# Two norms in front of cross attention: memory's norm is made earlier, and the squares of the second follow the residual chunk by chunk

## The chip, the cores and the metric

One core of a Trainium2 chip runs the whole program. The metric is the device time in microseconds (us) from the first to the last instruction of the slowest core, here of the only one. Five engines work side by side, each with its own instruction stream: TensorE (PE, matmuls into PSUM), VectorE (DVE), ScalarE (ACT), GpSimd (POOL, used here to issue some DMAs) and SyncE (SP, which issues the weight loads). They are kept in step by semaphores only.

## The reference

A layer of two blocks on 256 tokens of width 1024, in float32. The change touches the middle of the first block:

```python
merged = jax.nn.sigmoid(gate_ssd) * y_ssd + jax.nn.sigmoid(gate_mla) * y_mla   # y_mla = o @ w_mla_out
h = h + merged @ w_o[i]
h = h + memory_cross_attention(rms_norm(h, norm_xattn[i]), rms_norm(mem, norm_mem[i]), w_xq[i], w_xkv[i], w_xo[i])
...
def rms_norm(x, gain):
    xf = x * lax.rsqrt(jnp.mean(x * x, axis=-1, keepdims=True) + 1e-6)
    return xf * gain
...
q = h @ w_xq; k, v = jnp.split(mem @ w_xkv, 2, axis=-1)
```

Memory's norm (`n_mem`) doesn't depend on `h`. The norm of cross attention (`n_xattn`) needs the whole of `h` behind `w_o`.

## The kernel before

**Layout.** Activations are held turned: 128 partitions of the width by 8 tiles of the width by 256 tokens (`[128, 8, 256]`). The sum of squares of a norm thus runs over partitions, and a product with a matrix of ones makes it on TensorE (L514 in `norm_sum`), with the sum already spread to all partitions.

**Split weights.** Each weight comes in pieces of 128x2048 (256 output columns of a 1024-row matrix), loaded by SP into one of four `raw` buffers. ScalarE copies it to the reduced format (`whi`, L1325), VectorE subtracts (`wlo`, L1976), and TensorE makes three matmuls for each tile: high by high, high by low, low by high (L457 to L459; L490 to L492 in `chunks_late`). One chunk is 48 matmuls of 128x256. SP loads a piece when the piece four before it is split.

**Order.** Nothing is scheduled at run time: every engine's order is written out by hand, one Python function an engine. `upcoming(name, c)` makes the split of the piece two behind chunk c, on ScalarE and VectorE alike, so that both engines split weights in between their other work. An engine works strictly in its order; a wait stops all behind it.

**The stretch.** TensorE: four chunks of mla_out (the first by `chunks_late`), w_o 0 and 1 together by `chunks_late` (six of eight tiles of both, then the last two tiles, since these come from the last chunk of mla_out), the sum of `n_mem`, w_o 2 and 3, xk 0 (keys from the normed memory), the sum of `n_xattn`, xk 1 to 3, xq 0 to 3. For each chunk of mla_out VectorE multiplies by the gate (L2370), adds the SSD branch (L2372, `G`), ScalarE makes the high part (`MXh`), VectorE the low part (`MXl`, L1982). For each chunk of w_o VectorE adds it to the residual `H` (L2378).

**The norm's helper.** `norm` on ScalarE squares the lower half into `T8` (L1351), makes four gain products (L1325, `T8b`), later Ln and Exp of the sum (L1361, L1363; `table` loads another table set if need be, L1322), and the high part of the normed tiles. On VectorE it squares the upper half (L1991), adds the eight tiles in a tree down to one (L1998), makes the other four gain products (L2005), multiplies by the root (L2015) and makes the low part (L1982). `T8` is also `G2`, the MLA gate, and `T8b` holds keys of MLA, so `n_mem` can start only when the mixing is over; memT, too, is loaded by POOL only then, since its buffer overlaps others.

Of the kernel before, what the change touches and what calls it, by code (L numbers as in the profile page):

```python
# [4 lines left out]
F32 = mybir.dt.float32  # L5
# [3 lines left out]
ALU = mybir.AluOpType  # L9
# [215 lines left out]
def build(nc, I, out, parts, vectors):  # L225
# [36 lines left out]
    def R(name, shape, dt, offset):  # L262
        if name not in made:
            n = 4
            for s in shape[1:]:
                n *= s
            assert offset + n <= size, (name, offset + n, size)
            made[name] = sb(name, shape, dt, rbase + offset)
        return made[name]
# [104 lines left out]
    OAh, OAl = R("OAh", [128, 8, 256], F32R, 66 * KB), R("OAl", [128, 8, 256], F32R, 16 * KB)  # L374
    MXh, MXl = R("MXh", [128, 8, 256], F32R, 34 * KB), R("MXl", [128, 8, 256], F32R, 42 * KB)
    memT = R("memT", [128, 8, 256], F32, 8 * KB)
    MMh, MMl = R("MMh", [128, 8, 256], F32R, 16 * KB), R("MMl", [128, 8, 256], F32R, 24 * KB)
    XVh, XVl = R("XVh", [128, 8, 256], F32R, 32 * KB), R("XVl", [128, 8, 256], F32R, 40 * KB)
    q2, k2 = R("q2", [128, 8, 256], F32, 48 * KB), R("k2", [128, 8, 256], F32, 56 * KB)
# [57 lines left out]
    ru2 = ru[:, :].unsqueeze(1).broadcast_to([128, 2, 256])  # L437
    rh2 = rs[:, 256:512].unsqueeze(1).broadcast_to([128, 2, 256])
    rs2 = rs[:, 0:256].unsqueeze(1).broadcast_to([128, 2, 256])

    def halves(ps, a=2):
        return ps[:, :].rearrange("p (a n) -> p a n", a=a)
# [7 lines left out]
    def pe_program(pe):  # L450
# [56 lines left out]
        def norm_sum(nm, nt, ng=1, banks=bank):  # L507
            ps, free = banks.take(nm, "ms")
            v = T8[:, 0:ng * nt, :].rearrange("p (g k) n -> p g k n", g=ng)
            m = nt if nt % 2 else 1  # L510
            w.wait_ge(*free)
            w.wait_ge(*at_(nm, "squares"))
            for k in range(m):
                t = pe.matmul(ps[:, 0:256 * ng], ones[:, :], v[:, :, k, :], start=k == 0, stop=k == m - 1)  # L514
            t.then_inc(*did("norm_pe", nm, "ms"))
# [256 lines left out]
            chunk("mla_out", c, OAh, OAl, 8, lambda k: at_("emptied", "o", k // 2))  # L772


        def mem_side():
            yield
            norm_sum("n_mem", 8)

        side = mem_side()
        chunks_late("w_o", (0, 1), MXh, MXl, 8, lambda k: at_("mix", "lo", k // 2), 6)  # L780
        next(side)
        next(side, None)
        for c in range(2, 4):
            chunk("w_o", c, MXh, MXl, 8, lambda k: at_("mix", "lo", k // 2))

# [1 line left out]
        for c in range(4):  # L787
            chunk("xk", c, MMh, MMl, 8, lambda k: at_("n_mem", "lo", k // 4))
            if c == 0:
                norm_sum("n_xattn", 8)  # L790
        for c in range(4):
            chunk("xq", c, XVh, XVl, 8, lambda k: at_("n_xattn", "lo", k // 4))
        for j in range(2):
# [521 lines left out]
    def act_program(act):  # L1315
# [307 lines left out]
        for c in range(4):  # L1623
            upcoming("mla_out", c)
            w.wait_ge(*at_("mix", "sum", c))
            copy(MXh[:, 2 * c:2 * c + 2, :], G[:, 2 * c:2 * c + 2, :]).then_inc(*did("mix_act", "mix", "hi", c))

        def mem_side():
            yield from norm("n_mem", memT, 8, 1024, col["norm_mem"], ("dma", "mem"), [("mix", "lo", 3)], hs=MMh)

        side = mem_side()
        for c in range(4):
            upcoming("w_o", c)
            next(side, None)
        finish(side)


        side = norm("n_xattn", H, 8, 1024, col["norm_xattn"], ("emptied", "w_o", 3), [("n_mem", "lo", 1)], hs=XVh)
        next(side)
        for c in range(4):  # L1640
            upcoming("xk", c)
            evac(k2[:, 2 * c:2 * c + 2, :], "xk", c)
            next(side, None)
        finish(side)
        for c in range(4):
            upcoming("xq", c)
            evac(q2[:, 2 * c:2 * c + 2, :], "xq", c)
# [314 lines left out]
    def dve_program(dve):  # L1962
# [402 lines left out]
        for c in range(4):  # L2365
            upcoming("mla_out", c)
            f = slice(2 * c, 2 * c + 2)
            w.wait_ge(*at_("used", first["mla_out"] + c))
            w.wait_ge(*at_("mix", "sig2"))
            dve.tensor_tensor(G2[:, f, :], G2[:, f, :], halves(bank.ps("mla_out", c)), ALU.mult).then_inc(*bank.emptied("mla_out", c))  # L2370
            w.wait_ge(*at_("emptied", "mla_out", c))
            dve.tensor_tensor(G[:, f, :], G[:, f, :], G2[:, f, :], ALU.add).then_inc(*did("mix_dve", "mix", "sum", c))  # L2372
            w.wait_ge(*at_("mix", "hi", c))
            rest(MXl[:, f, :], G[:, f, :], MXh[:, f, :]).then_inc(*did("mix_dve", "mix", "lo", c))

        def residual(name, c):
            w.wait_ge(*at_("used", first[name] + c))
            dve.tensor_tensor(H[:, 2 * c:2 * c + 2, :], H[:, 2 * c:2 * c + 2, :], halves(bank.ps(name, c)), ALU.add).then_inc(*bank.emptied(name, c))  # L2378

        side = norm("n_mem", memT, 8, 1024, col["norm_mem"], T8b, ("dma", "mem"), [], hl=(MMh, MMl))  # L2380
        for c in range(4):
            upcoming("w_o", c)
            residual("w_o", c)
            next(side, None)
        finish(side)


        side = norm("n_xattn", H, 8, 1024, col["norm_xattn"], T8b, ("emptied", "w_o", 3), [], hl=(XVh, XVl))
        next(side)
        for c in range(4):  # L2390
            upcoming("xk", c)
            next(side, None)
        finish(side)
        for c in range(4):
            upcoming("xq", c)
        for j in range(2):
# [482 lines left out]
    def pool_program(pool):  # L2879
# [31 lines left out]
        pool.memset(kn[1][0:64, :, :], 0.0).then_inc(*did("mla_pool"))  # L2911
        w.wait_ge(*now("mla_pool"))
        pool.memset(kpm[:, :, :], 0.0).then_inc(*did("mla_pool", "mla", "zero"))
        w.wait_ge(*at_("mix", "lo", 3))
        pool.dma_start(memT[:, :, :], I["c_mem"].rearrange("p (k n) -> p k n", k=8)).then_inc(*did("mem", "dma", "mem", by=16))
        w.wait_ge(*at_("used", first["xv"] + 3))
        pool.dma_start(wr[:, :, :], I["c_router"].rearrange("p (k n) -> p k n", k=8)).then_inc(*did("router", "dma", "router", by=16))
# [91 lines left out]
```

## Time and profile before

| | |
|---|---|
| median of 3 runs | 1107.22 us (1103.17 to 1111.86) |
| the profiled execution, first to last instruction | 1106.8 us |
| mean granted TensorE clock | 0.974 of full speed |
| TensorE busy | 1021.5 us, 92% |
| VectorE busy | 622.6 us, 56% |
| ScalarE busy | 516.9 us, 47% |
| HBM read | 238.58 MB, 217 GB/s over the span |

The profile and the runs agree, so that a stretch of the trace can be added to or taken from the median. TensorE's share is the largest, but it is an average over stages; in some of them (the experts) it waits for weights.

### The profile page before, as it was taken

Reading aid. Unit: us, or ns where it says so; the run is one execution under the profiler, and the core shown is the slowest. Engines: PE = TensorE matmul, PEld = TensorE weight load, DVE = VectorE, ACT = ScalarE, POOL = GpSimd, SP = SyncE. Lnnn points to the kernel's source line nnn. Section 1 sums busy time; section 2 is a strip of 40 time slices with the busy share of each in tenths; the row PEclk is TensorE's granted clock in tenths of the full one; section 3 lists DMA queues with packets and bytes.
Section 4 is the critical chain, followed back from the end, with each engine's and each line's share of the span. In section 5 each row is a group of like instructions: output and inputs, shape, how many; then the busy total and the mean of one; then the engine's idle time right before and its main releaser. Section 6 shows DMA issues by size and latency. Waiting matters only on the chain.

```text
span 1106.8 us, 19429 instructions
## 1 busy us (share of the span) xinstructions
PE 1021.5 (92%) x8574; PEld 941.1 (85%) x8574; DVE 622.6 (56%) x828; ACT 516.9 (47%) x701; POOL 19.4 (2%) x24
## 2 busy tenths in 40 slices
PE   7999989899999899999997676788999999999998
PEld 6999978899889899899665443478999999999998
DVE  6887677765565784544111101068994665545566
ACT  5576576745555554442211110158566564443443
POOL 0000020001000000000000000000000000000000
PEclk9999999999999899998998888899999999999999
DMA  7665343446223555299999999964430355555441
GB/s 279 231 242 191 137 155 115 150 150 238 80 77 115 193 188 191 99 365 406 384 420 421 420 420 421 420 267 157 162 114 11 153 213 206 190 191 190 163 143 39
DMA packets 34871, 240.96 MB, mean 218 GB/s; under 512 B 4064, under 2 KB 4448, under 8 KB 6368
## 3 DMA queue, kind: packets, MB, share of 16 engines
q1 hardware_dynamic: 33264, 232.54, 55.1%
q0 software_dynamic: 1232, 6.99, 1.8%
q8 instruction: 70, 1.15, 0.4%
q10 hardware_dynamic: 288, 0.15, 0.1%
q14 instruction: 17, 0.14, 0.0%
HBM read 238.58 MB, written 1.08 MB: 217 GB/s over the span
## 4 chain that ended last, share of the span: by engine, by line
PE 68%; DVE 12%; DMA 9%; ACT 7%; issue 3%; SPq 2%; DVEq 0%; ACTq 0%
PE ps L457 15%; PE ps L459 15%; PE ps L458 15%; DVE wlo L1976 4%; PE ps L530 4%; PE ps L1226 4%; DMA xlo<-in_c_weights 3%; ACT whi L1325 3%; DMA xhi<-in_c_weights 3%; DMA wr<-in_c_weights 2%; PE ps L1192 2%; SPq L2933 2%; PE ps L1253 1%; PE ps L1266 1%; PE ps L929 1%
## 5 line engine op out<-in xcount | busy, mean ns | idle before, releaser
L1976 DVE TENSOR_TENSOR wlo<-raw,whi 128x2048 fp32r<-128x2048 f32 (+1 forms) x119 | 269.5, 2266 | 141.1 <-ACT whi L1325 141.1
L457 PE MATMUL ps<-XUh,whi 128*128 128x256 f32 x992 | 282.3, 285 | 9.2 <-DVE wlo L1976 8.4
L459 PE MATMUL ps<-XUh,wlo 128*128 128x256 f32 x992 | 278.3, 281 | 0.0
L458 PE MATMUL ps<-XUl,whi 128*128 128x256 f32 x992 | 278.2, 280 | 0.0
L1325 ACT ACTIVATE whi<-raw 128x2048 fp32r<-128x2048 f32 (+1 forms) x119 | 223.5, 1880 | 61.9 <-PE ps L459 61.9
L457 PEld LDWEIGHTS ps<-XUh,whi 128*128 128x128 f32 x992 | 187.3, 189 | 11.3 <-issue 7.7
L459 PEld LDWEIGHTS ps<-XUh,wlo 128*128 128x128 f32 x992 | 189.4, 191 | 0.0
L458 PEld LDWEIGHTS ps<-XUl,whi 128*128 128x128 f32 x992 | 187.5, 189 | 0.3
L1226 PE MATMUL ps<-wr,Xg 128*32 128x256 f32 x464 | 57.6, 433 | 6.2 <-DMA wr<-in_c_weights 4.6
L2855 DVE SCALAR_TENSOR_TENSOR sphs<-sphs,wsl,ps 128x256 f32<-128x256 f32 x8 | 3.8, 480 | 99.0 <-ACT sphs L1941 99.0
L1941 ACT ACTIVATE sphs<-ps 128x256 f32<-128x256 f32 x8 | 3.1, 383 | 102.1 <-PE ps L1226 102.1
L457 PE MATMUL ps<-ffnah,whi 128*128 128x256 f32 x176 | 49.4, 281 | 0.7 <-DVE wlo L1976 0.7
L459 PE MATMUL ps<-ffnah,wlo 128*128 128x256 f32 x176 | 49.1, 279 | 0.0
L458 PE MATMUL ps<-ffnal,whi 128*128 128x256 f32 x176 | 49.1, 279 | 0.0
L1226 PE MATMUL ps<-raw,Xg 128*32 128x256 f32 x208 | 37.9, 455 | 11.5 <-DMA wr<-in_c_weights 7.5
L1226 PEld LDWEIGHTS ps<-wr,Xg 128*32 128x32 f32 x464 | 29.5, 124 | 14.6 <-issue 9.2
L457 PE MATMUL ps<-YAh,whi 128*128 128x256 f32 x128 | 37.0, 289 | 2.3 <-DVE YAl L1982 2.3
L458 PE MATMUL ps<-YAl,whi 128*128 128x256 f32 x128 | 36.3, 284 | 0.0
L459 PE MATMUL ps<-YAh,wlo 128*128 128x256 f32 x128 | 36.3, 284 | 0.0
L1226 PEld LDWEIGHTS ps<-raw,Xg 128*32 128x32 f32 x208 | 17.5, 130 | 20.1 <-issue 17.2
L457 PEld LDWEIGHTS ps<-ffnah,whi 128*128 128x128 f32 x176 | 33.0, 188 | 0.8 <-issue 0.8
L459 PEld LDWEIGHTS ps<-ffnah,wlo 128*128 128x128 f32 x176 | 33.1, 188 | 0.0
(619 smaller groups left out, 2377.4 us busy)
## 6 DMA issues: line engine op xcount, KB each, us to landing
raw<-in_c_weights SPq DMA_DIRECT2D x141, 1024.0 KB, 4.9
wr<-in_c_weights SPq DMA_DIRECT2D x42, 1024.0 KB, 26.4
xhi<-in_c_weights SPq DMA_DIRECT2D x13, 1024.0 KB, 26.1
xlo<-in_c_weights SPq DMA_DIRECT2D x13, 1024.0 KB, 26.3
acb<-sums POOLq DMA_DIRECT2D x4, 1024.0 KB, 5.1
T<-in_c_weights SPq DMA_DIRECT2D x4, 1024.0 KB, 26.8
T8b<-in_c_weights SPq DMA_DIRECT2D x4, 1024.0 KB, 26.4
raw<-in_c_weights SPq DMA_DIRECT2D x4, 576.0 KB, 3.7
```

Source lines behind the costliest of these rows:

```text
L457: pe.matmul(ps, h(k), xh(k), start=start and k == 0, stop=False, skip_group_check=loose)
L458: pe.matmul(ps, h(k), xl(k), start=False, stop=False, skip_group_check=loose)
L459: t = pe.matmul(ps, l(k), xh(k), start=False, stop=stop and k == kt - 1, skip_group_check=loose)
L530: t = pe.matmul(ps[:, 256 * j:256 * j + 256], wt[:, k, 128 * j:128 * j + 128], x[:, k, :], start=n == j == 0, stop=n == 7, skip_group_chec ...
L929: t = pe.matmul(ps[:, 128 * hd:128 * hd + 128], x, x)
L1192: t = pe.matmul(ps[:, 128 * r:128 * r + 128], XT[:, j, 128 * k:128 * k + 128], Pg[:, j, :], start=j == 0, stop=j == 1)
L1226: t = pe.matmul(ps[o:o + 32, 256 * n:256 * n + 256], Xg[:, k, o:o + 32], plain_of(expert[name, 4 * g + e])[:, k, :], start=k == 0, stop=k ...
L1253: t = pe.matmul(dps[f][o:o + 32, :], aT[:, k, o:o + 32], plain_of(i)[:, k, 512 * f:512 * f + 512], start=k == 0, stop=k == 1)
L1266: t = pe.matmul(ps, Y[:, c], PT[:, :], start=g == 0 and d % 2 == 0, stop=False, skip_group_check=True)
L1325: return act.activation(out, in_, ACT.Copy, **kw)
L1976: dve.tensor_tensor(l[:, 0:n], r, h[:, 0:n].bitcast(F32), ALU.subtract).then_inc(*did("w_lo", "split", i))
L2933: sp.dma_start(raw_of(i), I["c_weights"][o:o + 128 * kt * n].rearrange("(p n) -> p n", p=128)).then_inc(*did("%s%d" % home[i], "loaded", i ...
```

## The change

- POOL issues memT's DMA behind the last transposes of MLA (`pT` 3) and not behind the last `MXl`.
- Two new tiles lie in the space of `XUh`, free once gate_mla is through: `memsq` for the squares of memory, `memg` for memory times its gain.
- ScalarE squares memory in mla_out's turns 0 and 1 (two 128x512 squares in each) and makes the eight gain products in turns 2 and 3 (four 128x256 in each). VectorE adds squares behind `MXl` in turns 1 and 2 (`add_square`, 128x512) and stops at two tiles.
- TensorE sums these two tiles by two products (`row_sum`), ahead of w_o 0 and 1. ScalarE takes the root ahead of the w_o loop and so of the split of w_o 2.
- In w_o's loop ScalarE makes memory's high part in turn 0, and in each turn c, behind the residual c, one square of 128x512 of `H` and two gain products. VectorE multiplies memory by the root in turn 0, makes its low part in turn 1, and adds squares of `H` in turns 2 and 3 and once behind the loop.
- The sum of `n_xattn` stays behind xk 0 and is two products as well. Its root, high and low part are made in the turns of xk 0 and xk 1.

```diff
 # tiles
+    memsq, memg = sb("memsq", [128, 8, 256], F32, xu_at), sb("memg", [128, 8, 256], F32, xu_at + 8 * KB)
 # TensorE
-        def mem_side():
-            yield
-            norm_sum("n_mem", 8)
-
-        side = mem_side()
+        def acc_sum(nm, acc):
+            ps, free = bank.take(nm, "ms")
+            w.wait_ge(*free)
+            row_sum(nm, ps[:, 0:256], acc).then_inc(*did("norm_pe", nm, "ms"))
+
+        acc_sum("n_mem", memsq)
         chunks_late("w_o", (0, 1), MXh, MXl, 8, lambda k: at_("mix", "lo", k // 2), 6)
-        next(side)
-        next(side, None)
...
             if c == 0:
-                norm_sum("n_xattn", 8)
+                acc_sum("n_xattn", T8)
 # ScalarE
             copy(MXh[:, 2 * c:2 * c + 2, :], G[:, 2 * c:2 * c + 2, :]).then_inc(*did("mix_act", "mix", "hi", c))
+            w.wait_ge(*at_("dma", "mem"))
+            w.wait_ge(*at_("used", first["gate_mla"] + 3))
+            if c < 2:
+                for j in (2 * c, 2 * c + 1):
+                    square("n_mem", memsq, memT[:, 2 * j:2 * j + 2, :], j)
+            else:
+                for k in range(4 * c - 8, 4 * c - 4):
+                    t = copy(memg[:, k, :], memT[:, k, :], scale=col["norm_mem"][:, k:k + 1])
+                t.then_inc(*did("norm_act", "n_mem", "gain", c - 2))
+
+        def upper(nm, hs, src):
+            for i in range(2):
+                w.wait_ge(*at_(nm, "dst", i))
+                copy(hs[:, 4 * i:4 * i + 4, :], src[:, 4 * i:4 * i + 4, :]).then_inc(*did("norm_act", nm, "hi", i))
+
+        root("n_mem", rs[:, 0:256], bank)
         for c in range(4):
             upcoming("w_o", c)
-            next(side, None)
+            if c == 0:
+                upper("n_mem", MMh, memg)
+            w.wait_ge(*at_("emptied", "w_o", c))
+            square("n_xattn", T8, H[:, 2 * c:2 * c + 2, :], c)
+            for k in (2 * c, 2 * c + 1):
+                t = copy(T8b[:, k, :], H[:, k, :], scale=col["norm_xattn"][:, k:k + 1])
+            t.then_inc(*did("norm_act", "n_xattn", "gain", c))
         for c in range(4):
             upcoming("xk", c)
             evac(k2[:, 2 * c:2 * c + 2, :], "xk", c)
-            next(side, None)
+            if c == 0:
+                root("n_xattn", rs[:, 256:512], bank)
+            if c == 1:
+                upper("n_xattn", XVh, T8b)
 # VectorE
             rest(MXl[:, f, :], G[:, f, :], MXh[:, f, :]).then_inc(*did("mix_dve", "mix", "lo", c))
+            if c == 1:
+                w.wait_ge(*at_("n_mem", "sq", 0))
+                add_square("n_mem", memsq, 1)
+            if c == 2:
+                add_square("n_mem", memsq, 2)
+                add_square("n_mem", memsq, 3)
...
         for c in range(4):
             upcoming("w_o", c)
+            if c == 0:
+                scale("n_mem", memg, rs4)
             residual("w_o", c)
-            next(side, None)
+            if c == 1:
+                lower("n_mem", MMl, memg, MMh)
+                w.wait_ge(*at_("n_xattn", "sq", 0))
+            if c > 1:
+                add_square("n_xattn", T8, c - 1)
+        add_square("n_xattn", T8, 3)
         for c in range(4):
             upcoming("xk", c)
+            if c == 1:
+                scale("n_xattn", T8b, rh4)
+                lower("n_xattn", XVl, T8b, XVh)
 # POOL
-        w.wait_ge(*at_("mix", "lo", 3))
+        w.wait_ge(*at_("pT", 3))
         pool.dma_start(memT[:, :, :], I["c_mem"].rearrange("p (k n) -> p k n", k=8)).then_inc(*did("mem", "dma", "mem", by=16))
```

`scale` multiplies by the root in two halves of 128x1024, `lower` subtracts the high part in two halves. `add_square`, `square`, `row_sum` and `root` are helpers of the kernel before, printed above where the diff calls them.

## Rows read from the trace of the kernel before

**Rows 1.** The page: busy time by engine, and the chain that ended last by engine

```profile
PE 1021.5 (92%) x8574; PEld 941.1 (85%) x8574; DVE 622.6 (56%) x828; ACT 516.9 (47%) x701; POOL 19.4 (2%) x24
...
PE 68%; DVE 12%; DMA 9%; ACT 7%; issue 3%; SPq 2%; DVEq 0%; ACTq 0%
```

**Rows 2.** Waits in 340 to 450: who waited for whom, us, times, longest

```profile
POOL memT L2915 <- DVE MXl L1982: 110.6, 1, 110.6
...
PE ps L514 <- DVE T L1998: 5.6, 2, 4.3
```

**Rows 3.** Windows: length, PE, PEld, DVE, ACT, POOL busy, granted clock, DMA share, GB/s

```profile
350.30:367.30 17.00, 17.00 (x147) 17.00 (x146) 12.48 (x12) 5.95 (x7) 0.00 (x0) 1.00 0.43 142
...
378.85:383.08 4.23, 0.00 (x0) 0.03 (x1) 3.71 (x5) 3.76 (x6) 0.00 (x0) 0.78 0.55 227
383.08:397.15 14.07, 14.07 (x98) 13.89 (x99) 11.39 (x9) 8.17 (x8) 0.00 (x0) 0.82 0.43 150
388.00:389.00 1.00, 1.00 (x10) 1.00 (x10) 1.00 (x1) 0.00 (x0) 0.00 (x0) 0.98 0.70 295
...
404.35:427.20 22.85, 22.85 (x192) 22.80 (x193) 16.98 (x10) 13.09 (x13) 0.00 (x0) 1.00 0.53 186
448.00:452.00 4.00, 4.00 (x20) 3.51 (x20) 2.68 (x4) 0.04 (x1) 0.00 (x0) 1.00 0.02 6
```

**Rows 4.** ScalarE in order of time: start, us, engine, line, what, idle before

```profile
354.58 1.90 ACT L1325 ACTIVATE whi<-raw 128x2048 fp32r<-128x2048 f32 x1
...
372.41 0.63 ACT L1325 ACTIVATE MXh<-G 128x512 fp32r<-128x512 f32 x1 [3.68 <-DVE G L2372]
372.94 1.90 ACT L1325 ACTIVATE whi<-raw 128x2048 fp32r<-128x2048 f32 x1
379.32 1.06 ACT L1351 ACTIVATE T<-memT 128x1024 f32<-128x1024 f32 x1 [4.48 <-DMA memT<-in_c_mem]
380.28 1.69 ACT L1325 ACTIVATE T8b<-memT,vec 128x256 f32<-128x256 f32 x4
381.88 1.89 ACT L1325 ACTIVATE whi<-raw 128x2048 fp32r<-128x2048 f32 x1
383.79 1.28 ACT L1322 ACT_TABLE_LOAD   x1
385.09 0.47 ACT L1361 ACTIVATE rs<-ps,small 128x256 f32<-128x256 f32 x1
...
385.92 1.89 ACT L1325 ACTIVATE whi<-raw 128x2048 fp32r<-128x2048 f32 x1
```

**Rows 5.** VectorE in order of time

```profile
356.52 2.29 DVE L1976 TENSOR_TENSOR wlo<-raw,whi 128x2048 fp32r<-128x2048 f32 x1 [1.11 <-ACT whi L1325]
...
366.95 0.69 DVE L1982 TENSOR_TENSOR MXl<-G,MXh 128x512 fp32r<-128x512 f32 x1 [0.70 <-ACT MXh L1325]
368.75 2.29 DVE L1976 TENSOR_TENSOR wlo<-raw,whi 128x2048 fp32r<-128x2048 f32 x1 [1.11 <-ACT whi L1325]
370.96 0.68 DVE L2370 TENSOR_TENSOR T<-T,ps 128x512 f32<-128x512 f32 x1
371.68 0.69 DVE L2372 TENSOR_TENSOR G<-G,T 128x512 f32<-128x512 f32 x1
...
392.32 2.35 DVE L2015 TENSOR_TENSOR T8b<-T8b,rs 128x1024 f32<-128x1024 f32 x2
```

**Rows 6.** The chain that ended last at memT's DMA; TensorE behind the second sum

```profile
374.07 5.17 DMA memT<-in_c_mem
...
404.35 0.67 PE L514 MATMUL ps<-T,ones 128*128 128x256 f32 x2 [1.36 <-DVE T L1998]
404.67 0.47 PE L457 MATMUL ps<-MMh,whi 128*128 128x256 f32 x1
```

**Rows 7.** A wait of TensorE in MLA, and a window behind it

```profile
333.13 0.46 PE L746 MATMUL ps<-PT,V 128*64 128x256 f32 x2 [2.33 <-ACT PT L1325]
...
334.00:336.00 2.00, 2.00 (x15) 1.44 (x12) 1.49 (x2) 1.51 (x3) 0.00 (x0) 0.50 0.00 0
```

More of the change, by code:

```diff
@@ L439, in build @@
     rs2 = rs[:, 0:256].unsqueeze(1).broadcast_to([128, 2, 256])
+    rs4, rh4 = (rs[:, o:o + 256].unsqueeze(1).broadcast_to([128, 4, 256]) for o in (0, 256))
     def halves(ps, a=2):
@@ L1626, in act_program @@
             copy(MXh[:, 2 * c:2 * c + 2, :], G[:, 2 * c:2 * c + 2, :]).then_inc(*did("mix_act", "mix", "hi", c))
-        def mem_side():
-            yield from norm("n_mem", memT, 8, 1024, col["norm_mem"], ("dma", "mem"), [("mix", "lo", 3)], hs=MMh)
-        side = mem_side()
+            w.wait_ge(*at_("dma", "mem"))
[12 more added lines that the diff above has]
+        root("n_mem", rs[:, 0:256], bank)
         for c in range(4):
             upcoming("w_o", c)
-            next(side, None)
-        finish(side)
-        side = norm("n_xattn", H, 8, 1024, col["norm_xattn"], ("emptied", "w_o", 3), [("n_mem", "lo", 1)], hs=XVh)
-        next(side)
+            if c == 0:
[5 more added lines that the diff above has]
+            t.then_inc(*did("norm_act", "n_xattn", "gain", c))
         for c in range(4):
@@ L1642, in act_program @@
             evac(k2[:, 2 * c:2 * c + 2, :], "xk", c)
-            next(side, None)
-        finish(side)
+            if c == 0:
+                root("n_xattn", rs[:, 256:512], bank)
+            if c == 1:
+                upper("n_xattn", XVh, T8b)
         for c in range(4):
@@ L2378, in residual, with scale, lower @@
             dve.tensor_tensor(H[:, 2 * c:2 * c + 2, :], H[:, 2 * c:2 * c + 2, :], halves(bank.ps(name, c)), ALU.add).then_inc(*bank.emptied(name, c))
-        side = norm("n_mem", memT, 8, 1024, col["norm_mem"], T8b, ("dma", "mem"), [], hl=(MMh, MMl))
+        def scale(nm, x, r4):
+            w.wait_ge(*at_(nm, "r"))
+            for i in range(2):
+                f = slice(4 * i, 4 * i + 4)
+                w.wait_ge(*at_(nm, "gain", i if nm == "n_mem" else 3))
+                dve.tensor_tensor(x[:, f, :], x[:, f, :], r4, ALU.mult).then_inc(*did("norm_dve", nm, "dst", i))
+        def lower(nm, l, x, h):
+            for i in range(2):
+                f = slice(4 * i, 4 * i + 4)
+                w.wait_ge(*at_(nm, "hi", i))
+                rest(l[:, f, :], x[:, f, :], h[:, f, :]).then_inc(*did("norm_dve", nm, "lo", i))
         for c in range(4):
             upcoming("w_o", c)
+            if c == 0:
+                scale("n_mem", memg, rs4)
             residual("w_o", c)
-            next(side, None)
-        finish(side)
-        side = norm("n_xattn", H, 8, 1024, col["norm_xattn"], T8b, ("emptied", "w_o", 3), [], hl=(XVh, XVl))
-        next(side)
+            if c == 1:
[4 more added lines that the diff above has]
+        add_square("n_xattn", T8, 3)
         for c in range(4):
             upcoming("xk", c)
-            next(side, None)
-        finish(side)
+            if c == 1:
+                scale("n_xattn", T8b, rh4)
+                lower("n_xattn", XVl, T8b, XVh)
         for c in range(4):
```

## The prediction

> **What bounds the kernel now.** I read the page first: TensorE is busy 92% of the span, and the chain that ended last is 68% TensorE with 12% VectorE, 9% DMA and 7% ScalarE [rows 1]. So only what TensorE waits for counts, and the question is which waits lie in the stretch that the diff touches (350 to 450 us) and what ends them. The list of waits names TensorE's own two: both are L514, the product that sums the squares of a norm, 5.6 us in total, and behind it stands the POOL queue, which issues the DMA of memT only after the last `MXl` [rows 2]. The windows then price them. TensorE runs without a gap from 350.3 to 378.85; it is empty until 383.08; it runs again, but the granted clock has fallen to its lower level of 1.2 GHz and returns at 388; a second gap of 1.36 us stands before `n_xattn`'s sum [rows 6]; from 404.35 to 427.2 it is full again [rows 3]. Full means 48 matmuls a chunk at 0.1177 us each, 5.65 us (three mla_out chunks take the 17.0 us of row 350.30).
>
> Next the other two engines, since the change moves work onto them. In the mla_out loop the two are not free, though their shares look low. ScalarE's `whi` of the next weight waits behind `MXh`, which waits for `G`, which on VectorE stands behind the `wlo` of the weight before. One turn is: `whi` to `wlo` 1.94 (354.58 to 356.52), `wlo` to the gate product 2.21 (368.75 to 370.96), from there to `G` 0.72, `G` to `MXh` 0.73, `MXh` to `whi` 0.53, together 6.13 us. The `wlo` rows 356.52 and 368.75 stand two turns of 6.12 apart [rows 4, 5]. TensorE's turn is 5.65 us. **The loop that looks half idle is a closed chain already slower than TensorE**; TensorE hides it only because the splits run ahead. w_o 1 is split at 368.75 + 2.29 = 371.04, and TensorE, in w_o 0 from 367.3, wants it 36 matmuls later at 371.5.
>
> **What is removed.** memT's DMA (5.2 us from issue to landing) moves from 374.07 to behind the last transposes of MLA [rows 6]. Between those and 350.3 lie two chunks (11.3) and the last value products, so it is issued near 338 and landed by 344, ten us before its first reader; POOL has nothing between, and behind it the DMA engines' share is 0.43 [rows 3], so I cost it at nothing. Were a weight late by it, `whi` would wait for its load, at most for its 5.2 us. The wait of 4.23 us goes, with it the slow clock after it: 383.08 to 397.15 is 14.07 us for one sum (0.5, below) and 96 matmuls (11.3), so the clock cost 2.3 us. The wait of 1.36 us before `n_xattn`'s sum would go too, if the squares kept up. Those are 7.9 us. VectorE also loses its squares, its gain product and the wide tree additions, but where they stood TensorE was waiting or VectorE had time.
>
> **What is added on TensorE.** Each sum becomes two products instead of one. L514 has two records for one product, 0.67 us together [rows 6]; less the tail that any matmul lays over the next (0.28 - 0.12) that is 0.5 us. So +0.5 twice, 1.0 us. The gain is then at most 7.9 - 1.0 = 6.9 us.
>
> **What is added to the chain.** Prices from rows 4: a square of 128x512 isn't there; the copy `MXh` of the same shape from SBUF is 0.63 us, 0.53 to the next start; half of L1351 (1.06 for 128x1024, 0.96 to the next start) gives 0.48. Bounds are 0.40 (a 128x256 step) and 0.63 (no overlap). Four gain copies take 1.60 to the next start (380.28 to 381.88).
> Turn 0: two squares in front of `whi`, +1.06. Turn 1: two more, +1.06, 2.12 in all. So `MXl` of turn 2 starts at 366.95 + 2.12 = 369.07. Behind it VectorE makes the additions 2 and 3 (a 128x512 addition like `G`, 0.69; the second waits for the first): 369.67 and 370.39, done 371.08. **The new order on TensorE puts `n_mem`'s sum ahead of w_o 0 and 1**, which are ready at 367.3. What is queued behind this wait is 96 matmuls that need nothing from it. TensorE idles 367.3 to 371.1, 3.8 us: the removed wait is back, 11 us earlier, for another reason.
> Turns 2 and 3: four gain copies each, +1.60 each. `MXh` of turn 3 comes at 372.41 + 2.12 + 1.60 = 376.13; then 0.53, the copies 1.60, and the root, which now stands in front of `whi` of w_o 2: table load 1.30, Ln 0.50, Exp 0.33 (383.79 to 385.92). `whi` of w_o 2 starts at 380.39; before it was 372.94. Split at 380.39 + 1.94 + 2.29 = 384.6. TensorE, from 371.1, has 1.0 + 11.3 and arrives at 383.4: 1.2 us idle.
> w_o loop: behind that split VectorE scales memory (L2015's two halves, 2.35), then the residual 0 (a 128x512 operation like the gate product, 386.84 to 387.52). ScalarE makes both upper halves (until 387.9), a square 0.53 and two gains 0.80, and `whi` of w_o 3 starts at 389.3; split at 393.5. TensorE finished w_o 2 at 390.3: 3.2 us idle. From here each turn is `whi` 1.94, `wlo` 2.21, residual 0.71, square 0.53, gains 0.80, 6.19 us, again closed, since the gains of chunk c stand before the `whi` of the weight after next. `whi` of xk 0 at 395.5, split 399.7 (idle 0.5); `whi` of xk 1 at 401.7; residual 3 at 405.85, its square at 406.56, the last addition 407.2 to 407.9. TensorE ended xk 0 at 405.4, so 2.5 us idle, then the two products. xk 1 starts at 408.9. Before it started at 404.67 [rows 3, 6].
>
> The sum: waits 3.8 + 1.2 + 3.2 + 0.5 + 2.5 = 11.2 and four products 2.0, 13.2 us, against 5.6 + 1.0 + 2.3 = 8.9 before, +4.3; the two starts give **+4.2 us**, which I take. Eight squares stand in the chain; with steps of 0.40 or 0.63 instead of 0.53 it is +3.2 or +5.0. Behind xk 1 nothing changes: carried on by the same durations, the splits of xk 2, xk 3 and `XVl` fall at 412, 415 and 420 against needs at 414.4, 420 and 425.7, TensorE is full, and later DMAs start from events that move along (in 448 to 452 the DMA share is 0.02) [rows 3]. So the shift reaches the end whole.
>
> On the table load row 383.79 shows 1.28 us and the Ln starts 0.02 us later, and that is what I used. The Trainium skill (ScalarE: Activation LUTs, "What ACT_TABLE_LOAD costs") adds a drain, about 2.66 us in all, to a switch. As the root now stands in the chain, that would make the sum +5.6 instead of +4.2; this trace does not show the drain.
>
> **Rivals.**
> A, a gain: the added work on ScalarE and VectorE fits in their idle time. For it speaks that both are idle a third of the loop and more, that all squares are off TensorE and that the DMA is out of the way. Then xk 1 starts at 367.3 + 1.0 + 22.6 + 5.65 + 1.0 = 397.55, 7.1 us earlier: 1100.1 us. Against it speaks the 6.12 us turn. It can come true only in part, by as much as ScalarE gets ahead; the idle 3.68 us before each `MXh` ends with `G`, thus with the chain itself. Half of it would be 1103.7.
> B, slower through the clock: the lower level after waits. A wait of 2.33 us was followed by a stretch at 0.50 of full speed, the one of 4.23 by a longer one, that of 1.36 by none [rows 3, 6, 7]. Here 3.8, 3.2 and 2.5 us waits stand in a row. The first two cost little, for TensorE waits for splits behind them anyway (a slow w_o 3 would end by 402 and xk 0 with the sum's due time). The place that decides is the wait of 2.5 us before `n_xattn`'s sum: behind it TensorE is the bound, and a stretch at half clock there is not hidden. Price by the stretch of before 2.3 us: +6.5, 1113.7 us. If the clock slows w_o 3, this last wait shrinks to some 1.3 us and the fall may not come, which is why B is not my forecast.
> On rule B the Trainium skill (TensorE: Matmul & The Clock Gate, "HAM oscillation — how this bites in real kernels") says that waits in each tile bring the slow clock back each time; the rows here agree for the longer waits and not for the one of 1.36.
> C, the change doesn't act (the sum's wait stays where the DMA ended it): excluded by the order of the POOL queue; I give it nothing of its own.
>
> **How the numbers follow.** The profiled execution spans 1106.8 us, the median of the runs is 1107.22 (1103.17 to 1111.86), so the two agree and I add to the median: 1107.2 + 4.2 = 1111.4. Chances: forecast (+3 to +5.5) 0.52; B, with whatever small misses lengthen the chain (+5.5 to +9), 0.22; a partial gain or nothing (-4 to +3) 0.12; A whole 0.07; worse than +9, by a chain that I don't see, 0.07. One per cent, 11 us, is about what a measurement of this kernel can tell from no change. A whole is -0.7%, so even there faster by over 1% needs luck: 0.04. Over +11 us: 0.06. The rest 0.90. The range for 8 in 10 leaves out A and the worst: 1102 to 1117.
>
> **What would show it.** In the profile after: memT landing near 344; TensorE empty from about 367 to 371 and released by a VectorE addition; `wlo` rows 7.2, 7.2, 7.7 us apart in the mla_out loop instead of 6.12, and three waits of L457 for `wlo`, of which that for w_o 3 is over 3 us; then about 2.5 us before the second sum; xk 1 at 408 to 409. If instead the wait at 367 is under 1 us, my closed turn is wrong and A holds. If all starts agree and the time is longer, it is the granted clock behind 408. What would make all of it wrong is a release that I put on the wrong instruction, above all whether `whi` really stands behind the squares in ScalarE's order.

## The result and the profile after

The changed kernel takes 1111.35 us (median of 20 runs, 1104.64 to 1116.53), the kernel before in the same rounds 1105.32 us: a ratio of 1.0042, 95% interval 1.0025 to 1.0058. The change makes the kernel slower by 0.4%, which is 4.6 us with an interval of 2.8 to 6.4 us. (The two medians alone stand 6.0 us apart.) The profiled execution of the changed kernel spans 1111.7 us, against 1106.8.

The page first (busy time by engine, then the chain that ended last). TensorE is busy 3.2 us longer and ScalarE 5.7 us, VectorE 5.9 us less. These totals over the whole span don't say where the 4.9 us of span come from; ScalarE's part of the last chain rises from 7% to 9% [rows 1].

```profile
PE 1024.7 (92%) x8578; PEld 942.5 (85%) x8578; DVE 616.7 (55%) x824; ACT 522.6 (47%) x715; POOL 19.4 (2%) x24
...
PE 65%; DVE 12%; DMA 11%; ACT 9%; issue 3%; SPq 1%; DVEq 0%; ACTq 0%
```

Who waited for whom in 340 to 450, the answer to [rows 2] (L539 is the matmul of `row_sum`, which takes L514's place; L459 is the former L457, L1993 the former L1976):

```profile
DVE wlo L1993 <- ACT whi L1326: 43.2, 17, 4.9
...
PE ps L539 <- DVE memsq L2054: 3.8, 1, 3.8
...
PE ps L539 <- DVE T L2054: 2.3, 1, 2.3
...
PE ps L459 <- DVE wlo L1993: 1.5, 1, 1.5
```

Both sums still wait, and a wait for a split weight has joined them. VectorE's waits for `whi` stood at 29.3 us in this list before (15 times) and are now 43.2 us (17 times): the additional work of ScalarE is seen there, though two more waits are in the count. Windows of the same stretch, the answer to [rows 3]:

```profile
366.07:369.83 3.76, 0.01 (x1) 0.03 (x1) 2.78 (x5) 2.90 (x6) 0.00 (x0) 0.91 0.82 279
369.83:376.00 6.17, 6.17 (x25) 5.81 (x26) 4.27 (x4) 2.49 (x5) 0.00 (x0) 0.50 0.28 77
376.00:382.80 6.80, 6.80 (x59) 6.80 (x59) 1.86 (x1) 4.85 (x7) 0.00 (x0) 1.00 0.20 84
382.80:390.74 7.94, 7.94 (x68) 7.74 (x66) 4.29 (x5) 5.25 (x6) 0.00 (x0) 1.00 0.38 134
390.74:392.20 1.46, 0.00 (x1) 0.03 (x1) 1.46 (x2) 0.00 (x0) 0.00 (x0) 1.00 0.00 0
...
404.32:406.66 2.34, 0.00 (x1) 0.03 (x1) 2.09 (x4) 1.51 (x4) 0.00 (x0) 1.00 0.54 102
406.66:410.20 3.54, 3.54 (x13) 3.18 (x14) 1.79 (x1) 3.51 (x5) 0.00 (x0) 0.52 0.55 229
```

Read the columns PE and PEclk together. TensorE is empty for 3.76 us ahead of w_o, then works 6.2 us at half clock; it is empty for 1.46 us before w_o 3 and for 2.34 us before the second sum, and then works at half clock again for some 3.4 us. ScalarE in order of time, the answer to [rows 4], shows the turns of mla_out:

```profile
352.62 0.63 ACT L1326 ACTIVATE MXh<-G 128x512 fp32r<-128x512 f32 x1 [3.69 <-DVE G L2389]
353.15 1.14 ACT L1376 ACTIVATE memsq<-memT 128x512 f32<-128x512 f32 x2
354.19 1.90 ACT L1326 ACTIVATE whi<-raw 128x2048 fp32r<-128x2048 f32 x1
359.78 0.63 ACT L1326 ACTIVATE MXh<-G 128x512 fp32r<-128x512 f32 x1 [3.68 <-DVE G L2389]
...
366.93 0.63 ACT L1326 ACTIVATE MXh<-G 128x512 fp32r<-128x512 f32 x1 [3.68 <-DVE G L2389]
...
374.64 0.63 ACT L1326 ACTIVATE MXh<-G 128x512 fp32r<-128x512 f32 x1 [3.68 <-DVE G L2389]
375.18 1.69 ACT L1326 ACTIVATE memg<-memT,vec 128x256 f32<-128x256 f32 x4
376.89 1.28 ACT L1323 ACT_TABLE_LOAD   x1
378.18 0.47 ACT L1381 ACTIVATE rs<-ps,small 128x256 f32<-128x256 f32 x1
378.69 0.42 ACT L1383 ACTIVATE rs<-rs 128x256 f32<-128x256 f32 x1
379.01 1.90 ACT L1326 ACTIVATE whi<-raw 128x2048 fp32r<-128x2048 f32 x1
```

The squares take 1.04 us from their start to that of `whi`, the four gain products behind the third `MXh` 1.59, and **the idle time before each `MXh` is still 3.68 us**. ScalarE was idle for 3.68 us a turn, took on 1.0 to 1.6 us of work a turn, and is idle for 3.68 us a turn: the turn has become longer by the work. That is the mark of a closed chain. VectorE's rows say the same, the answer to [rows 5] (`wlo` at 348.96, 356.13, 363.29, 370.99; turns of 7.17, 7.16 and 7.70 us instead of 6.12):

```profile
348.96 2.29 DVE L1993 TENSOR_TENSOR wlo<-raw,whi 128x2048 fp32r<-128x2048 f32 x1 [4.34 <-ACT whi L1326]
...
356.13 2.29 DVE L1993 TENSOR_TENSOR wlo<-raw,whi 128x2048 fp32r<-128x2048 f32 x1 [2.15 <-ACT whi L1326]
...
363.29 2.29 DVE L1993 TENSOR_TENSOR wlo<-raw,whi 128x2048 fp32r<-128x2048 f32 x1 [1.55 <-ACT whi L1326]
...
368.21 1.48 DVE L2054 TENSOR_TENSOR memsq<-memsq 128x512 f32<-128x512 f32 x2
370.99 2.29 DVE L1993 TENSOR_TENSOR wlo<-raw,whi 128x2048 fp32r<-128x2048 f32 x1 [1.30 <-ACT whi L1326]
```

The chain that ended last, in order of time, runs through exactly these instructions between 360 and 371, with no TensorE in it:

```profile
360.31 1.14 ACT memsq L1376 x2
361.45 1.81 ACT whi L1326
363.26 0.02 issue
363.29 2.29 DVE wlo L1993
365.58 0.60 DVE T L2387
366.19 0.02 issue
366.21 0.70 DVE G L2389
```

**One stretch for all comparisons.** Runs of one kernel differ by up to 1%, and what happens ahead of 350 us is not the change's doing, so I compare by a stretch: from the start of the first `MXh` to the start of ScalarE's eviction of xk 1, the first point behind which TensorE is again the bound. Before it is 410.71 - 354.05 = 56.66 us, after 415.06 - 352.62 = 62.44 us: +5.8 us in this execution, of which 1.7 is the fall of the clock behind the second sum (half of 3.4 us). The other 4.1 are what the longer waits, the two further products and the slow clock behind the first wait add. The span shows 4.9, since in this execution the changed kernel reached the first `MXh` 1.4 us earlier. It was 0.9 us ahead at 21 us already and gained another 0.5 near 213 us, where its clock stayed at full speed while that of before fell behind a wait of 2.3 us. The code there is the same. Behind xk 1 both have the same way to go (696.1 and 696.6 us).

### The profile page after: what moved, and what is told of

Its sections match the earlier page's. It is cut to its first block, busy times and chain, and to the rows that moved or that the text cites. A ratio compares the mean times of both kernels' runs of the same rounds, so it can differ in the third digit from the quotient of the medians.

```text
span 1111.7 us, 19448 instructions
## 1 busy us (share of the span) xinstructions
PE 1024.7 (92%) x8578; PEld 942.5 (85%) x8578; DVE 616.7 (55%) x824; ACT 522.6 (47%) x715; POOL 19.4 (2%) x24
## 4 chain that ended last, share of the span: by engine, by line
PE 65%; DVE 12%; DMA 11%; ACT 9%; issue 3%; SPq 1%; DVEq 0%; ACTq 0%
PE ps L459 15%; PE ps L461 14%; PE ps L460 14%; DMA raw<-in_c_weights 6%; DVE wlo L1993 5%; PE ps L532 4%; PE ps L1227 3%; ACT whi L1326 3%; DMA xhi<-in_c_weights 3%; DMA wr<-in_c_weights 2%; PE ps L1193 1%; PE ps L930 1%; PE ps L1254 1%; PE ps L1267 1%; PE ps L825 1%
## 5 line engine op out<-in xcount | busy, mean ns | idle before, releaser
L1993 DVE TENSOR_TENSOR wlo<-raw,whi 128x2048 fp32r<-128x2048 f32 (+1 forms) x119 | 269.6, 2267 | 154.3 <-ACT whi L1326 154.2
L459 PE MATMUL ps<-XUh,whi 128*128 128x256 f32 x992 | 281.4, 284 | 8.8 <-DVE wlo L1993 8.2
L459 PEld LDWEIGHTS ps<-XUh,whi 128*128 128x128 f32 x992 | 186.6, 188 | 10.7 <-issue 7.4
L1227 PE MATMUL ps<-wr,Xg 128*32 128x256 f32 x464 | 55.3, 426 | 6.6 <-DMA wr<-in_c_weights 4.7
L459 PE MATMUL ps<-ffnah,whi 128*128 128x256 f32 x176 | 49.4, 281 | 0.7 <-DVE wlo L1993 0.7
L1227 PE MATMUL ps<-raw,Xg 128*32 128x256 f32 x208 | 37.3, 450 | 13.3 <-DMA wr<-in_c_weights 9.2
L459 PE MATMUL ps<-YAh,whi 128*128 128x256 f32 x128 | 36.3, 284 | 2.8 <-DVE YAl L1999 2.2
L459 PEld LDWEIGHTS ps<-ffnah,whi 128*128 128x128 f32 x176 | 33.0, 188 | 0.8 <-issue 0.8
```

Source lines behind the costliest of these rows:

```text
L459: pe.matmul(ps, h(k), xh(k), start=start and k == 0, stop=False, skip_group_check=loose)
L1227: t = pe.matmul(ps[o:o + 32, 256 * n:256 * n + 256], Xg[:, k, o:o + 32], plain_of(expert[name, 4 * g + e])[:, k, :], start=k == 0, stop=k ...
L1993: dve.tensor_tensor(l[:, 0:n], r, h[:, 0:n].bitcast(F32), ALU.subtract).then_inc(*did("w_lo", "split", i))
```

## The experiments

Times of different rounds lie up to 5 us apart for one kernel, so ratios to the kernel before in the same rounds are given (8 to 12 runs of each experiment, 20 of the changed kernel); the stretch is that just defined, from the one profiled execution of each. Where the clock fell behind the last wait in that execution (changed, e2, e5, e9), the stretch holds some 1.7 us for it.

| kernel | ratio to before (95%) | stretch, us |
|---|---|---|
| before | 1 | 56.66 |
| changed | 1.0042 (1.0025 to 1.0058) | 62.44 |
| e1: memory's work ahead of the wait | 0.9991 (0.9965 to 1.0017) | 55.76 |
| e2: sum behind w_o 0 and 1 | 1.0090 (1.0055 to 1.0124) | 65.78 |
| e3: before, with the early DMA | 0.9987 (0.9959 to 1.0015) | 55.82 |
| e4: rearranged | 0.9927 (0.9902 to 0.9951) | 49.15 |
| e5: changed, first wait filled | 1.0042 (1.0022 to 1.0062) | 62.38 |
| e6: changed, last wait filled | 1.0025 (1.0005 to 1.0045) | 61.23 |
| e7: memory part alone | 0.9994 (0.9970 to 1.0017) | 56.81 |
| e8: rearranged, one product a sum | 0.9928 (0.9904 to 0.9952) | 49.10 |
| e9: rearranged in memory's part only | 0.9999 (0.9981 to 1.0016) | 55.07 |
| e10: changed, squares doubled | a single run, 1114.29 us | 62.90 |
| e11: e1, squares doubled | a single run, 1107.47 us | 55.77 |

**e1: memory's squares and gains ahead of the wait for the mix sum.**

```diff
             upcoming("mla_out", c)
-            w.wait_ge(*at_("mix", "sum", c))
-            copy(MXh[:, 2 * c:2 * c + 2, :], G[:, 2 * c:2 * c + 2, :]).then_inc(*did("mix_act", "mix", "hi", c))
             w.wait_ge(*at_("dma", "mem"))
             w.wait_ge(*at_("used", first["gate_mla"] + 3))
             if c < 2:
...
                 t.then_inc(*did("norm_act", "n_mem", "gain", c - 2))
+            w.wait_ge(*at_("mix", "sum", c))
+            copy(MXh[:, 2 * c:2 * c + 2, :], G[:, 2 * c:2 * c + 2, :]).then_inc(*did("mix_act", "mix", "hi", c))
```

> The changed kernel with one thing moved: in mla_out's turns ScalarE makes memory's squares and gain products ahead of its wait for the mix sum (where it sat idle 3.68 us in each turn) and not behind the high part of the mix. Same work, same sums, same place of the sum on TensorE. Closed chain (my theory): the turns fall back from 7.2, 7.2, 7.7 us to 6.12; the wait before n_mem's sum shrinks from 3.8 to about 1.7 us, the start of xk 1 comes 5.2 us earlier than in the changed kernel, so about 1.2 us earlier than before the change: ratio to before 0.999, with 2.5 us still waited before the second sum. Rival, the place of the sum on TensorE: the place is the same, so the time stays at +4 to +5 us over before. Rival, the amount of work on ScalarE and VectorE: the same, so also +4 to +5.

Measured: ratio 0.9991; the `wlo` rows stand 6.12, 6.13 and 6.32 us apart, the wait before the sum is 1.68 us:

```profile
370.01 1.10 PE L539 MATMUL ps<-memsq,ones 128*128 128x256 f32 x4 [1.68 <-DVE memsq L2054]
```

The same instructions, swapped with one copy and its wait, take the whole loss away: the interval of e1 ends at 1.0017, that of the changed kernel begins at 1.0025. Of the 6.7 us of stretch between the two, 1.7 is the fall of the clock, which did not come in e1's execution; 5.0 are left, against 5.2 expected. Neither the amount of work nor the place of the sum, which are the same in both, makes the loss by itself.

**e2: the sum back to its old place on TensorE.**

```diff
-        acc_sum("n_mem", memsq)
         chunks_late("w_o", (0, 1), MXh, MXl, 8, lambda k: at_("mix", "lo", k // 2), 6)
+        acc_sum("n_mem", memsq)
```

> The changed kernel with n_mem's sum moved on TensorE behind w_o 0 and 1, where it was before the change; ScalarE's order stays, with the root ahead of the split of w_o 2. Closed chain: the wait of 3.8 us goes, but the root now ends near 385 and with it every later split comes later; TensorE waits over 5 us for w_o 2 and 3.3 us for w_o 3, xk 1 starts 3.5 us later than in the changed kernel: +7.5 to +9 us over before, ratio 1.007 to 1.008. Rival, the place of the sum on TensorE: the wait of 3.8 us is gone and nothing replaces it, +0 to +1 us over before.

Measured: ratio 1.0090, stretch +3.3 us on the changed kernel. The place of the sum looks like the culprit in the list of waits (3.8 us, the longest), and moving it makes things worse. Its removal uncovers the next release: ScalarE's root now waits for the sum and holds up `whi` of w_o 2 behind it, from 379.01 to 382.26, and TensorE waits 6.6 us for two splits: 5.14 us for w_o 2, and 1.45 for w_o 3 where 3.3 were expected, with a stretch at half clock in between. ScalarE of e2 in order of time:

```profile
376.75 1.28 ACT L1323 ACT_TABLE_LOAD   x1
381.43 0.47 ACT L1381 ACTIVATE rs<-ps,small 128x256 f32<-128x256 f32 x1 [3.40 <-PE ps L539]
381.94 0.42 ACT L1383 ACTIVATE rs<-rs 128x256 f32<-128x256 f32 x1
382.26 1.89 ACT L1326 ACTIVATE whi<-raw 128x2048 fp32r<-128x2048 f32 x1
```

**e3: the early DMA alone, in the kernel before.**

```diff
-        w.wait_ge(*at_("mix", "lo", 3))
+        w.wait_ge(*at_("pT", 3))
         pool.dma_start(memT[:, :, :], I["c_mem"].rearrange("p (k n) -> p k n", k=8)).then_inc(*did("mem", "dma", "mem", by=16))
```

> The kernel before with one line of the change: memT is loaded behind the last transposes of MLA. Its norm still runs in w_o's loop. My reckoning: the squares start at 378.1 (VectorE, behind the residual) instead of 379.3, the sum 1.1 us earlier, the wait 3.1 instead of 4.2 us, and nothing is late by the earlier load: -1 us, ratio 0.999; with the clock falling for 3.4 instead of 6.8 us it is up to -2.7. Rival, the early load costs by contention with weights: 0 or slower than before.

Measured: ratio 0.9987, stretch -0.84 us, the waits for both sums 4.4 us instead of 5.6. One line of the change, taken alone, costs nothing; that it gains in time stays within the interval, the stretch shows its size.

**e4: the same work rearranged.** ScalarE's loop over mla_out and over w_o, and VectorE's additions:

```diff
             upcoming("mla_out", c)
+            if c == 0:
+                w.wait_ge(*at_("dma", "mem"))
+                w.wait_ge(*at_("used", first["gate_mla"] + 3))
+                for j in range(4):
+                    square("n_mem", memsq, memT[:, 2 * j:2 * j + 2, :], j)
+            elif c < 3:
+                for k in range(4 * c - 4, 4 * c):
+                    t = copy(memg[:, k, :], memT[:, k, :], scale=col["norm_mem"][:, k:k + 1])
+                t.then_inc(*did("norm_act", "n_mem", "gain", c - 1))
+            else:
+                root("n_mem", rs[:, 0:256], bank)
             w.wait_ge(*at_("mix", "sum", c))
             copy(MXh[:, 2 * c:2 * c + 2, :], G[:, 2 * c:2 * c + 2, :]).then_inc(*did("mix_act", "mix", "hi", c))
...
-        root("n_mem", rs[:, 0:256], bank)
         for c in range(4):
             upcoming("w_o", c)
+            if c:
+                follow(c - 1)
             if c == 0:
                 upper("n_mem", MMh, memg)
-            w.wait_ge(*at_("emptied", "w_o", c))
-            square("n_xattn", T8, H[:, 2 * c:2 * c + 2, :], c)
...
+        follow(3)
```

`follow(c)` is the wait for residual c, its square and its two gains. On VectorE the additions stand behind turns 0 and 1.

> All of the change's work in other places of ScalarE's and VectorE's order: the four squares of memory ahead of the wait for the mix sum in turn 0, the gain products in turns 1 and 2, the root in turn 3; VectorE's three additions behind turns 0 and 1; in w_o's loop the square and gains of residual c stand behind the split made in turn c+1. Closed chain: no wait is left between 350 and xk 1, xk 1 starts 11.4 us earlier than in the changed kernel, 7.3 us earlier than before: ratio to before 0.993 (0.992 to 0.995). Rival, the amount of work: it is the same as in the changed kernel, so +4 to +5 us. Rival, the place of the sum on TensorE (unchanged): its wait ends when the squares end, so a gain of at most 3.8 us on the changed kernel: 0.

Measured: ratio 0.9927. **TensorE waits for nothing between 350 and xk 1's end**, the granted clock is 1.00 throughout, and the stretch is 7.5 us shorter than before (7.3 expected) and 13.3 shorter than in the changed kernel (11.4 expected, which left out the clock fall of 1.7 behind the changed kernel's last wait). ScalarE of e4 in the first turns; the work lies in front of `MXh`, and the idle time has shrunk by it, as it should where work is covered:

```profile
349.40 2.18 ACT L1376 ACTIVATE memsq<-memT 128x512 f32<-128x512 f32 x4
353.18 0.63 ACT L1326 ACTIVATE MXh<-G 128x512 fp32r<-128x512 f32 x1 [1.60 <-DVE G L2396]
353.71 1.90 ACT L1326 ACTIVATE whi<-raw 128x2048 fp32r<-128x2048 f32 x1
355.52 1.69 ACT L1326 ACTIVATE memg<-memT,vec 128x256 f32<-128x256 f32 x4
359.30 0.63 ACT L1326 ACTIVATE MXh<-G 128x512 fp32r<-128x512 f32 x1 [2.09 <-DVE G L2396]
```

**e5 and e6: products of ones in a wait, to hold the clock.** They add work that nobody reads, in front of one of the sums:

```diff
             w.wait_ge(*free)
+            if nm == "n_mem":                                   # e5; e6: "n_xattn" and 9 products
+                constant_products(pe, ps[:, 384:512], 14)
             row_sum(nm, ps[:, 0:256], acc).then_inc(*did("norm_pe", nm, "ms"))
```

> The changed kernel with 14 products of ones (128x128) on TensorE in its first wait (3.8 us), ahead of n_mem's sum, into an unused part of the bank; nothing reads them. They take some 3.1 us and keep TensorE's clock from falling. Theory: the time that the slow clock costs behind the first wait is hidden, since TensorE waits for the splits of w_o 2 and 3 anyway; the waits that the slow clock had swallowed come back (about 1.2 us before w_o 2, 3.2 us before w_o 3) and xk 1 starts where it did: no change against the changed kernel, ratio to before 1.004. Rival, the clock is the cost: w_o 0 to 2 run at full speed, some 2.3 us are saved at the end, ratio 1.002.

Measured: ratio 1.0042, the same as the changed kernel, stretch 62.38. The clock stayed at full speed through w_o, as this window of e5 shows (PEclk 1.00 where the changed kernel had 0.50), and the time that this saved came back as waits for splits.

```profile
367.50:376.00 8.50, 8.50 (x69) 8.40 (x70) 4.27 (x4) 4.79 (x8) 0.00 (x0) 1.00 0.35 125
```

These waits are 4.1 us in all instead of 1.5, the one before w_o 3 is 2.98 us instead of 1.46, as TensorE's row of e5 has it:

```profile
389.93 0.36 PE L459 MATMUL ps<-MXh,whi 128*128 128x256 f32 x1 [2.98 <-DVE wlo L1995]
```

Here the slow clock in front of a later wait cost nothing.

> The changed kernel with 9 products of ones (128x128, about 2.0 us) in the last of its waits (2.3 us, before n_xattn's sum). Behind this wait TensorE is the bound, and the profile after showed 3.4 us at 1.2 GHz there. If that fall is a cost of its own: 1.7 us less than the changed kernel from the last high part of the mix to the end of xk 1 (60.8 us instead of 62.4), ratio to before 1.0027 against 1.0042. If the fall cost nothing: no change.

Measured: stretch 61.23 instead of the 60.8 expected (w_o 3 ran at half clock in this execution, xk 0 ended 0.8 us later, and the products, 2.17 us, ran 0.5 us over the sum's due time), ratio 1.0025 against 1.0042. The intervals of the two overlap, so in time it is not shown; in the stretch 1.2 of the 1.7 us are back, with no fall behind the sum. The profiled executions show the price directly: from the start of xk 0's eviction to that of xk 1's it is 6.78, 6.71 and 6.72 us where the clock fell (changed, e5, e9) and 5.16, 5.16 and 5.17 where it didn't (e1, e10, e11), behind the same wait of 2.34 us. A slow clock behind the last wait does cost.

**e7: memory's part alone.** n_xattn's norm is that of before (`norm` on ScalarE and VectorE, `norm_sum` on TensorE):

```diff
-                acc_sum("n_xattn", T8)
+                norm_sum("n_xattn", 8)
...
-            w.wait_ge(*at_("emptied", "w_o", c))
-            square("n_xattn", T8, H[:, 2 * c:2 * c + 2, :], c)
...
+        side = norm("n_xattn", H, 8, 1024, col["norm_xattn"], ("emptied", "w_o", 3), [("n_mem", "lo", 1)], hs=XVh)
...
```

> The memory part of the change alone; n_xattn's norm as before (squares behind the whole residual, a tree, one product). Closed chain: the wait of 3.8 us and the split of w_o 2 stay as in the changed kernel, but w_o's turns lose the square and the gains (1.33 us a turn), the wait for w_o 3's split is 1.9 instead of 3.3, the wait before the second sum 0.9, xk 1 starts 3.9 us earlier than in the changed kernel: ratio to before 1.000 to 1.001. Thus both halves of the change cost about the same. Rival, only the place of n_mem's sum costs: the time stays at 1.004.

Measured: ratio 0.9994, stretch 56.81, 5.6 us less than the changed kernel (3.9, and no clock fall, as the last wait is 0.63 us). The wait of 3.76 us before n_mem's sum is still there, so a kernel with that wait in full is as fast as the one before. Put on top of e7, the residual's part of the change, squares in front of the next split, brings 5.6 of the 5.8 us (1.7 of them the fall of the clock); the equal halves of the expectation did not come. But e1 takes as much away by touching memory's part alone. The waits stand in a row, so the parts don't add up to shares of the loss.

**e8: the rearranged kernel with one product a sum.** VectorE adds the two remaining tiles (`last_add`, 128x256) and TensorE makes one product of the result.

> The rearranged kernel (memory's work ahead of the waits, residual squares one split later) with each sum as one product, VectorE adding the last two tiles first (128x256, 0.44 us, in its slack). If a product costs 0.5 us of TensorE where nothing else waits: 1.0 us less than the rearranged kernel, ratio to before 0.992. If VectorE's additional addition makes a wait, it shows before L539's place: then no gain.

Measured: ratio 0.9928, stretch 49.10, no gain. TensorE saves 0.43 us at the first sum (from its start to w_o 0's first product 0.24 us instead of 0.67) and then waits 0.57 us for w_o 3's split, where it waited for nothing. VectorE's rows show why. Here is turn 1 of e4:

```profile
360.57 1.48 DVE L2061 TENSOR_TENSOR memsq<-memsq 128x512 f32<-128x512 f32 x2
361.97 2.28 DVE L2000 TENSOR_TENSOR wlo<-raw,whi 128x2048 fp32r<-128x2048 f32 x1
```

and here the same place in e8:

```profile
359.85 1.48 DVE L2062 TENSOR_TENSOR memsq<-memsq 128x512 f32<-128x512 f32 x2
361.37 0.42 DVE L2068 TENSOR_TENSOR memsq<-memsq 128x256 f32<-128x256 f32 x1
361.71 2.29 DVE L2001 TENSOR_TENSOR wlo<-raw,whi 128x2048 fp32r<-128x2048 f32 x1
```

In e4 VectorE has no idle time before this `wlo`. In e8 it therefore starts 9.26 us behind the first `MXh` instead of 8.79, and the `wlo` of w_o 3 28.99 instead of 28.51. The added 0.42 us lie in the closed chain and make it longer. The second sum saves its 0.44 us (from its start to xk 1's eviction 6.28 us instead of 6.72), which make up for that and no more.

**e9: only memory's part rearranged.** As e4, but the squares and gains of the residual stay ahead of the next split.

> Between the changed and the rearranged kernel: memory's squares, gain products and root ahead of the waits as in the rearranged one, but in w_o's loop the square and gains of residual c still ahead of the split of the next weight, as in the changed one. Closed chain: no wait before n_mem's sum and w_o 2; w_o's turns stay at 6.2 us, so waits of about 1.0 us for w_o 3, 0.5 for xk 0 and 2.5 before the second sum stay, xk 1 starts 7.3 us earlier than in the changed kernel and 4.1 later than in the rearranged one; from the first high part of the mix to the end of xk 1 53.4 us, and 55.1 if the clock falls behind the last wait; ratio to before 0.997. Rival, what is left of the cost lies in memory's part alone: as fast as the rearranged kernel, 0.993.

Measured: ratio 0.9999, stretch 55.07 (55.1 expected with the clock fall, which came), waits 1.0, 0.3 and 2.34 us. The ratio is above the 0.997 that I expected. That had left out the fall, which is 1.7 us or 0.0015, about half of the miss; 0.9985 lies in the interval, and the rest stays open. Against e4 one difference is left, the place of `follow`, and it is worth 5.9 us of stretch, 1.7 of them the fall of the clock. The `wlo` rows of w_o's loop in e9 stand 6.27 and 6.19 us apart (378.01, 384.28, 390.47), nearly as those of the changed kernel do (6.27 and 6.20): w_o's loop is a second closed chain.

**e10 and e11: each of memory's squares made twice,** behind `MXh` (as in the change) and ahead of the wait (as in e1):

```diff
                 for j in (2 * c, 2 * c + 1):
+                    act.activation(memg[:, 2 * j:2 * j + 2, :], memT[:, 2 * j:2 * j + 2, :], ACT.Square)
                     square("n_mem", memsq, memT[:, 2 * j:2 * j + 2, :], j)
```

> The changed kernel with each of memory's four squares made twice (the additional one into a tile that is overwritten later), in the same place, behind the high part of the mix. Closed chain: each additional square of 0.53 lengthens the chain by itself, two in turn 0 and two in turn 1, 2.1 us: the wait before n_mem's sum is 5.9 us instead of 3.8, the end of xk 1 at 64.5 us from the first high part instead of 62.4. Rival, ScalarE has idle time for it (3.68 us in each turn): no change.

Measured: turns of 8.2, 8.2 and 7.7 us (`wlo` at 346.90, 355.11, 363.31, 371.01), the wait before the sum 5.8 us. The start of xk 0's eviction is 57.74 us from the first `MXh` against 55.66 in the changed kernel, +2.08, as expected. The end of xk 1 is at 62.90, only +0.46: behind the same last wait of 2.34 us the clock did not fall this time (1.00 from 406.67 to 410).

> The same doubled squares in the kernel with memory's work ahead of the wait for the mix sum. Closed chain: four squares, 2.1 us, still fit in the 3.68 us: turns stay at 6.12 us, the wait before n_mem's sum stays 1.7 us, the end of xk 1 at 55.8 us from the first high part, as without them. Rival, the amount of work on ScalarE: 2.1 us later.

Measured: 55.77 us against 55.76 in e1. The same four squares cost 2.1 us behind the high part and nothing in front of the wait. ScalarE's idle time before the first two `MXh` tells the two apart: it is 3.68 us in e10, as without the additional squares, and 1.60 in e11, where e1 has 2.64 and 2.65.

## Why the prediction was right

The forecast was 1111.4 us with xk 1 4.2 us later; it came to 1111.35 and a ratio of 1.0042. That the two times agree to 0.05 us is luck. The forecast was added to a median of 1107.22, and the same kernel measures 1105.32 in the rounds of the result: against that the changed kernel is 6.0 us slower by the medians and 4.6 (2.8 to 6.4) by the ratio. In the profiled execution xk 1 starts 55.48 us behind the first `MXh` instead of 50.62, +4.9. What was right is the chain and the size of its cost. Point by point:

- **The closed turn.** The step on which all hangs, that ScalarE's idle 3.68 us in front of `MXh` are not free for work placed behind it, is shown by e1, by the doubled squares of e10 and e11 and by the `wlo` rows at 7.17, 7.16 and 7.70 us (7.2, 7.2, 7.7 forecast). Prices: two squares took 1.04 to 1.05 us (1.06 forecast from `MXh`), the four gains 1.59, the switch with the root 2.12.
- **The first wait** came as computed, 3.76 us (3.8), released by VectorE's addition.
- **The waits behind it.** Forecast were 1.2 before w_o 2, 3.2 before w_o 3 and 0.5 before xk 0; seen were none, 1.46 and 0.33, so the sign given for w_o 3, over 3 us, did not come. The clock fell to 1.2 GHz behind the first wait for 6.8 us, made w_o 0 to 2 later and so filled the waits. e5, without the fall, has the others: 4.1 us in two, 2.98 of them before w_o 3. That these two exchange without changing the time was a step of rival B, and e5 shows it.
- **The last wait** 2.34 us (2.5). From the first `MXh` on, the second sum starts at 54.04 us; forecast were 407.9 - 354.05 = 53.85.
- **Rival B.** The text gave it as less likely, since a slow w_o 3 would shrink the last wait. In the profiled execution w_o 3 ran at full clock, the last wait stayed long and the clock fell behind it (in e6's it was the other way round): 1.7 us instead of the 2.3 of its price. The cost over 20 runs, 4.6 us with an interval of 2.8 to 6.4, fits the 4.2 without the fall as well as the 5.8 of the profiled execution. How often the fall comes in them was not measured.
- **Rival A** was refuted for this order of instructions and is true of another one. It was priced at 1100.1 us, 0.9936 of before; e4, with the same work, measures 0.9927. Its reasoning on the amount of idle time was sound; what failed it was the place of the work, as the prediction had it. The prediction's sentence that it could come true only in part holds for the change, not for the kernel.
- **The removed DMA wait, at nothing for the early load:** it landed in 7.7 us instead of 5.2, near 344, and held up nobody; e3 shows it alone.
- **The table switch** cost what its row shows: 1.28 us and 0.01 to the Ln, in the chain (376.89 to 378.18). The drain of which the Trainium skill speaks (ScalarE: Activation LUTs, "What ACT_TABLE_LOAD costs"), which by the prediction's estimate would have made it +5.6, did not appear: the page's figure doesn't hold here.
- **The second product of each sum** was priced at 0.5 us. e4 and e8 differ by it and show 0.43 us at the first sum and 0.44 at the second, at full clock. e8 gained nothing since VectorE's addition, put in its place, stands in the closed chain.

Not tried was the residual's part alone on the kernel before; its share follows from e7 and e9 by subtraction only.

## What to carry to other kernels

Idle time in front of a wait is free only for work placed in front of that wait. Put the same work behind the instruction that the wait guards, and in a loop in which two engines release each other, as here, the turn gets longer by all of it, while the idle time in the profile stays as it was: an engine that took on work and is idle exactly as long as before sits in such a chain. Work given to the other engine of such a loop is no better off where that engine has no idle time left, as the 0.42 us of VectorE in e8 show. Before moving a product that waits, as in e2, look at who waits for its result; the longest wait in the list need not be the one that sets the end.

## What the runs showed of the hardware

The same wait of TensorE, 2.34 us before the second sum, was followed by a stretch of about 3.4 us at 1.2 GHz in the profiled executions of the changed kernel, e5 and e9, and by none in those of e1, e10 and e11. One execution so differs from another by 1.7 us at a single place, in kernels with the same instructions around it. The first wait, 3.75 or 3.76 us, came with 6.8 us at the lower level in the changed kernel, and with 3.4 us in e6 and e7. A longer wait didn't mean a longer fall: 3.04 us in e3, 4.23 in the kernel before and 5.83 in e10 came with 6.8 us, 5.14 in e2 with 3.4. A profile of one execution thus gives the cost of the clock behind a wait of 2 to 4 us only to within some 2 us.
